# A two-block transformer kernel: order of the ScalarE and VectorE queues inside its two feed-forward stages

## The chip, the cores and the metric

The kernel runs on one core of one Trainium2 chip. The metric is the device time of one execution in microseconds (us), and the median of three runs is taken. TensorE multiplies, ScalarE (ACT in the profile), VectorE (DVE) and GpSimd (POOL) work elementwise, and SyncE (SP) issues most of the transfers. Each engine works through its own instruction queue in order, and the queues meet only at semaphores.

## The reference

Two transformer blocks work on 512 tokens of width 1024 (and 16 meta tokens), in float32. Each block has attention layers, an output projection and a feed-forward part. The change lies in the feed-forward part alone, which is the same in both blocks:

```
hn = rms_norm(h, g)
h  = h + (silu(hn @ w_gate) * (hn @ w_up)) @ w_down      # 1024 -> 2816 -> 1024
```

## The kernel before, in words

**Tiles.** Activations are kept with features on the 128 partitions and the 512 tokens along the free axis. The 2816 inner features are 22 tiles of 128, done in three parts of 8, 8 and 6 tiles (`FPARTS`): part a, b, c. After each part the product with `w_down` adds what the part gives to `hT` (phases `dn1a` and so on).

**Split operands.** A float32 product is done as three products of a rounded high half and a remainder: `wh` and `wl` of the weights, high and low half of the activations. ScalarE makes `wh` from the loaded weights in `stage` (`high`, L767). VectorE subtracts it to make `wl` (`low`, L1170). `stage`, `wh` and `wl` have two slots, b = 0 and 1. SyncE loads the next tile into a slot when `lo[b]` says that `wl` of the tile in it is made. TensorE starts `product(name, i, b)` (L1951) when `wl` of that tile is made and PSUM bank b has been read (`ev[b]`). ScalarE may overwrite `wh[b]` when the last product from it has ended (`mm[b]`).

**Ordinary tiles.** The first four inner tiles of part a in each block (`GATE_PLAIN`) are ordinary. Slot 0 holds the gate tile and slot 1 the up tile, and each product is 24 matmuls of 128x512. VectorE scales the gate product by the norm factor `R` (L1682), ScalarE takes the tanh (L1008), VectorE closes the silu (`opened`, L1649), scales the up product (L1654) and multiplies both (L1656). ScalarE makes the high half of the inner tile (`inner_high`, L995) and VectorE its low half (`inner_low`, L1661). In tile 0 the norm factor itself is made: VectorE waits for sums from TensorE, takes an inverse square root in small steps (L1600 to L1202) and builds four diagonals, from which TensorE spreads the factor.

**Gate pairs.** All other gate tiles are done in pairs (`gate_pair`, L1997), two gate tiles and then two up tiles; there are 2, 4 and 3 pairs in parts a, b and c, so 18 in both blocks. The two gate tiles over two halves of the tokens are multiplied by a scheme with seven half products instead of eight. It uses sums of weight tiles (`weight_sums`, L1627 to L1631, split by `sum_high` L979 and `sum_low` L1639) and sums of token halves (`token_sum` L1610, split by `token_sum_high` L990 and `token_sum_low` L1617; four of them for each block, made while the ordinary tiles run, into two scratch tiles `ta` and `tb`). The order on TensorE of the half products, each 12 matmuls of 128x256, is in this text x1, w, z, y1, x2, y2, x3. The banks x and y (`psS` 0 and 2) are used again within a pair, so ScalarE has to copy their interim sums out: `part_x` after x1 (L1032) and after x2 (L1040), `part_z` after z (L1035) and after y1 (L1038). y2 waits for the copy made after y1 (`out_y`), and x3 for the copy made after x2 (`out_x`). Then follow the two up tiles as ordinary products. `second_high` (L985) and `second_low` (L1644) are the second half of the split of a pair's second gate tile.

**The queue of ScalarE in a pair before the change:**

```python
act.activation(part_x[:, 0:HT], psS[:, 0, 0:HT], ACT.Copy).then_inc(out_x, 1)    # after x1
high(name, i + 1, 0)                                                             # first up tile
act.activation(part_z[:, 0:HT], psS[:, 3, 0:HT], ACT.Copy).then_inc(out_z, 1)    # after z
high(name, i + 1, 1)                                                             # second up tile
act.wait_ge(acc_y, 2 * n + 1)
act.activation(part_z[:, HT:], psS[:, 2, 0:HT], ACT.Copy).then_inc(out_y, 1)     # after y1
act.wait_ge(acc_x, 3 * n + 2)
act.activation(part_x[:, HT:], psS[:, 0, 0:HT], ACT.Copy).then_inc(out_x, 1)     # after x2
```

The order of all of this is written out by hand, in `swiglu` of the scalar block (L997) and `swiglu` of the vector block (L1663).

Of the kernel before, what the change touches and what calls it, by code (L numbers as in the profile page):

```python
# [235 lines left out]
def build(nc, t, out):  # L236
    with ExitStack() as ctx:
# [150 lines left out]
        ft, o = at("ft", [P, 5, SEQ], o)  # L388
# [366 lines left out]
        def _(act):  # L755
# [241 lines left out]
            def swiglu(l, part):  # L997
                name, f0, pairs_ = f"gu{l}{'abc'[part]}", before_part(l, part), gate_pairs(l, part)
                plain = GATE_PLAIN[part]
                for i in range(plain):  # L1000
                    high(name, i, 1)
                    if i == 0:
                        high_next(name, i, False)
                    if i == 1:
                        token_sum_high(l, 0)
                        token_sum_high(l, 1)
                    act.wait_ge(ev[0], PAIR0[name] + i + 1)
                    act.activation(ft[:, 1, :], ft[:, 0, :], ACT.Tanh, scale=0.5).then_inc(t_ok, 1)  # L1008
                    if i:
                        high_next(name, i, False)  # L1010
                    if i == 1:
                        token_sum_high(l, 2)
                        inner_high(i, f0)
                    elif i == 2:
                        token_sum_high(l, 3)
                        inner_high(i, f0)
                    elif i == plain - 1:
                        sum_high(pairs_[0][1], 0)
                        second_high(name, pairs_[0][0])
                        inner_high(i, f0)  # L1020
                        sum_high(pairs_[0][1], 1)
                    else:
                        inner_high(i, f0)
                if not plain:
                    sum_high(pairs_[0][1], 0)
                    second_high(name, pairs_[0][0])
                    sum_high(pairs_[0][1], 1)

                for i, n in pairs_:
                    last = i == pairs_[-1][0]  # L1030
                    act.wait_ge(acc_x, 3 * n + 1)
                    act.activation(part_x[:, 0:HT], psS[:, 0, 0:HT], ACT.Copy).then_inc(out_x, 1)  # L1032
                    high(name, i + 1, 0)
                    act.wait_ge(mm[1], PAIR0[name] + i + 1)
                    act.activation(part_z[:, 0:HT], psS[:, 3, 0:HT], ACT.Copy).then_inc(out_z, 1)  # L1035
                    high(name, i + 1, 1)
                    act.wait_ge(acc_y, 2 * n + 1)
                    act.activation(part_z[:, HT:], psS[:, 2, 0:HT], ACT.Copy).then_inc(out_y, 1)  # L1038
                    act.wait_ge(acc_x, 3 * n + 2)
                    act.activation(part_x[:, HT:], psS[:, 0, 0:HT], ACT.Copy).then_inc(out_x, 1)  # L1040
                    act.wait_ge(gate_ok, 2 * n + 1)
                    act.activation(ft[:, 1, :], ft[:, 0, :], ACT.Tanh, scale=0.5).then_inc(t_ok, 1)
                    act.wait_ge(gate_ok, 2 * n + 2)
                    act.activation(tanh2[:], ft[:, 2, :], ACT.Tanh, scale=0.5).then_inc(t_ok, 1)
                    if not last:
                        sum_high(n + 1, 0)
                    high_next(name, i + 1, last)
                    inner_high(i, f0)
                    if not last:
                        sum_high(n + 1, 1)  # L1050
                        second_high(name, i + 2)
                    inner_high(i + 1, f0)
# [9 lines left out]
            name = "dn1c"  # L1062
# [44 lines left out]
            for j in range(len(units) + 6):  # L1107
# [4 lines left out]
                if j in Y_NORM:  # L1112
                    i = Y_NORM.index(j)
# [18 lines left out]
            name = "dn2c"  # L1132
# [24 lines left out]
        def _(v):  # L1157
# [490 lines left out]
                v.wait_ge(t_ok, f0 + i + 1)  # L1648
                dv.link(v.scalar_tensor_tensor(out=gated, in0=tanh, scalar=1.0, in1=gated, op0=ALU.add, op1=ALU.mult))  # L1649

            def times_up(name, i, b, up, f0, gated):

                done(name, up, b)
                v.tensor_tensor(ft[:, 3, :], psL[:, b, :], R, ALU.mult).then_inc(ev[b], 1)  # L1654
                v.wait_ge(ev[b], PAIR0[name] + up + 1)
                v.scalar_tensor_tensor(out=ft[:, 4, :], in0=gated, scalar=0.5, in1=ft[:, 3, :], op0=ALU.mult, op1=ALU.mult).then_inc(hid_ok, 1)  # L1656

# [5 lines left out]
            def swiglu(l, part, head=None):  # L1663
                name, f0, pairs_ = f"gu{l}{'abc'[part]}", before_part(l, part), gate_pairs(l, part)
                first, pair0 = pairs_[0]
                for i in range(first):
                    low(name, i, 1)
                    if i == 0:
                        new_rms(head[0])
                        diagonals(diag, rs[:, 0:4]).then_inc(diag_ok, 1)  # L1670
                        low_next(name, i, False)
                        v.wait_ge(bcast, head[1])
                        v.tensor_copy(R, psT[:, 1, :]).then_inc(R_ok, 1)
                        v.wait_ge(R_ok, head[1])
                    if i == 1:
                        token_sum(l, 0)
                        token_sum(l, 1)
                    elif i == 2:
                        token_sum_low(l, 1)
                        token_sum(l, 3)  # L1680
                    done(name, i, 0)
                    v.tensor_tensor(ft[:, 0, :], psL[:, 0, :], R, ALU.mult).then_inc(ev[0], 1)  # L1682
                    if i:
                        low_next(name, i, False)
                    opened(i, f0, ft[:, 0, :], ft[:, 1, :])
                    if i == 1:
                        token_sum_low(l, 0)
                        token_sum(l, 2)
                    elif i == 2:
                        token_sum_low(l, 2)  # L1690
                        token_sum_low(l, 3)
                    elif i == first - 1:
                        weight_sums(name, first, pair0)
                        sum_low(pair0, 0)
                        second_low(name, first)
                    times_up(name, i, 1, i, f0, ft[:, 0, :])
                    inner_low(i, f0)
                    if i == first - 1:
                        sum_low(pair0, 1)

                for i, n in pairs_:
                    last = i == pairs_[-1][0]
                    done(name, i, 0)
                    v.wait_ge(out_x, 2 * n + 1)
                    v.tensor_tensor(ft[:, 0, 0:HT], psS[:, 1, 0:HT], part_x[:, 0:HT], ALU.add).then_inc(ev[0], 1)
                    low(name, i + 1, 0)
                    low(name, i + 1, 1)
                    v.wait_ge(acc_y, 2 * n + 2)
                    v.wait_ge(out_x, 2 * n + 2)
                    dv.link(v.tensor_tensor(ft[:, 0, HT:], psS[:, 2, 0:HT], part_x[:, HT:], ALU.add))  # L1710
                    v.tensor_tensor(ft[:, 0, :], ft[:, 0, :], R, ALU.mult).then_inc(gate_ok, 1)
                    v.wait_ge(acc_x, 3 * n + 3)
                    v.wait_ge(out_y, n + 1)
                    v.wait_ge(out_z, n + 1)
                    v.tensor_tensor(ft[:, 2, :].rearrange("p (a t) -> p a t", a=2), psS[:, 0, 0:HT].unsqueeze(1).broadcast_to([P, 2, HT]),
                                    part_z[:].rearrange("p (a t) -> p a t", a=2), ALU.add).then_inc(ev[1], 1)
                    v.wait_ge(ev[1], PAIR0[name] + i + 1)
                    v.tensor_tensor(ft[:, 2, :], ft[:, 2, :], R, ALU.mult).then_inc(gate_ok, 1)
                    v.wait_ge(gate_ok, 2 * n + 2)
                    opened(i, f0, ft[:, 0, :], ft[:, 1, :])  # L1720
                    opened(i + 1, f0, ft[:, 2, :], tanh2[:])
                    if not last:
                        weight_sums(name, i + 2, n + 1)
                    times_up(name, i, 0, i + 1, f0, ft[:, 0, :])
                    low_next(name, i + 1, last)
                    if not last:
                        sum_low(n + 1, 0)
                    inner_low(i, f0)
                    if not last:
                        sum_low(n + 1, 1)  # L1730
                    times_up(name, i + 1, 1, i + 1, f0, ft[:, 2, :])
                    if not last:
                        second_low(name, i + 2)
                    inner_low(i + 1, f0)
# [750 lines left out]
```

## Time and profile before

| | |
|---|---|
| median of three runs | 1555.14 us (1549.74 to 1555.39) |
| the profiled execution, its own time | 1557.15 us |
| its span, first to last instruction | 1555.4 us |
| TensorE busy with matmuls, with weight loads | 97%, 81% |
| VectorE, ScalarE, GpSimd busy | 62%, 39%, 16% |
| mean granted TensorE clock | 0.994 |

Busy time is the time in which an engine works on instructions. The idle time before an instruction is put down to what released it. Matmuls are pipelined and the ends that the profile gives for them are modelled, so starts are the safer reading.

### The profile page before, as it was taken

To read this page: it belongs to the slowest core of one execution; us is meant where nothing else is said; L and a number is where in the kernel's file an instruction comes from. 1 tells how busy PE (TensorE), PEld (TensorE's weight loads), DVE (VectorE), ACT (ScalarE), POOL (GpSimd) and SP (SyncE) were. 2 spreads that over 40 slices of the span, in tenths; PEclk is the share of its full clock that TensorE was granted. 3 is DMA by queue.
4 is the path that set the end of the run, shared out by engine and by line. 5 is a ranking of instruction groups with operands and counts; after the bars stand their busy time and mean duration, and the time that the engine had idled before them with its cause. 6 is when DMAs were issued, how large, how long until landed. Compare 5 with 4: busy or idle time off the path is not lost.

```text
span 1555.4 us, 21898 instructions
## 1 busy us (share of the span) xinstructions
PE 1508.1 (97%) x8004; PEld 1253.4 (81%) x8004; DVE 968.6 (62%) x1698; ACT 607.0 (39%) x1061; POOL 241.9 (16%) x206
## 2 busy tenths in 40 slices
PE   7999999999989999999999999999999999999998
PEld 6878886877778888888799778788777788888886
DVE  5578795466676477476854283544657855863764
ACT  5134445524433244243511374444343423432433
POOL 2323334340000000000002553222400000000000
PEclk9999999999999999999999999999999999999999
DMA  6524420033333333332323202111332233333322
GB/s 150 150 56 150 124 55 1 8 100 99 92 95 88 99 91 104 95 96 85 91 82 86 63 1 82 55 57 38 104 93 86 85 103 107 87 95 95 109 68 95
DMA packets 250308, 132.96 MB, mean 85 GB/s; under 512 B 21226, under 2 KB 247654, under 8 KB 250223
## 3 DMA queue, kind: packets, MB, share of 16 engines
q1 hardware_dynamic: 247998, 123.92, 28.0%
q0 software_dynamic: 2144, 7.77, 1.6%
q8 instruction: 54, 0.88, 0.2%
q14 instruction: 32, 0.25, 0.1%
q10 hardware_dynamic: 80, 0.14, 0.0%
HBM read 129.67 MB, written 6.38 MB: 87 GB/s over the span
## 4 chain that ended last, share of the span: by engine, by line
PE 77%; DVE 10%; DMA 6%; ACT 4%; issue 2%; POOL 0%; SPq 0%; DVEq 0%; ACTq 0%; POOLq 0%
PE psL L1971 44%; PE psL L2151 11%; PE psS L1971 5%; PE psS L1994 4%; DMA stage<-in_w_ffn_up 2%; ACT wh L767 2%; PE psT L2160 2%; DMA stage<-in_w_ff_up 2%; PE psS L2407 1%; DVE wl L1170 1%; PE psL L2279 1%; PE psS L2430 1%; DVE ft L1654 1%; PE psS L2256 1%; DVE ft L1656 1%
## 5 line engine op out<-in xcount | busy, mean ns | idle before, releaser
L767 ACT ACTIVATE wh<-stage 128x1024 fp32r<-128x1024 f32 (+3 forms) x232 | 225.3, 971 | 378.3 <-PE psL L1971 248.6
L1971 PE MATMUL psL<-hn,wh 128*128 128x512 f32 x1104 | 350.3, 399 | 7.9 <-DVE wl L1170 7.3
L1971 PEld LDWEIGHTS psL<-hn,wh 128*128 128x128 f32 x1104 | 204.1, 188 | 59.2 <-DVE wl L1170 11.4
L1170 DVE TENSOR_TENSOR wl<-stage,wh 128x1024 fp32r<-128x1024 f32 (+1 forms) x151 | 180.3, 1194 | 81.0 <-ACT wh L767 80.8
L1971 PE MATMUL psL<-hid,wh 128*128 128x512 f32 x704 | 221.6, 395 | 1.2 <-DVE wl L1170 1.2
L1971 PE MATMUL psL<-hn,wl 128*128 128x512 f32 x552 | 217.3, 394 | 0.0
L617 POOL TENSOR_TENSOR wl<-stage,wh 128x1024 fp32r<-128x1024 f32 (+2 forms) x81 | 154.4, 1907 | 306.9 <-ACT wh L767 306.9
L2151 PE MATMUL psL<-hn,wh 128*128 128x512 f32 x496 | 173.0, 430 | 0.4 <-DVE yn L1885 0.4
L1971 PEld LDWEIGHTS psL<-hid,wh 128*128 128x128 f32 x704 | 131.3, 187 | 35.2 <-DVE wl L1170 2.8
L1971 PE MATMUL psL<-hid,wl 128*128 128x512 f32 x352 | 138.8, 394 | 0.0
L1971 PEld LDWEIGHTS psL<-hn,wl 128*128 128x128 f32 x552 | 103.9, 188 | 23.8
L2151 PEld LDWEIGHTS psL<-hn,wh 128*128 128x128 f32 x496 | 88.7, 189 | 19.3 <-DVE yn L1885 0.8
L2151 PE MATMUL psL<-hn,wl 128*128 128x512 f32 x248 | 97.9, 395 | 0.0
L1739 DVE TENSOR_TENSOR hT<-hT,psL 128x512 f32 (+1 forms) x48 | 32.9, 686 | 93.7 <-PE psL L1971 93.6
L1971 PE MATMUL psS<-hn,wh 128*128 128x264 f32 x448 | 87.3, 296 | 0.7 <-DVE hn L1220 0.7
L1971 PE MATMUL psL<-mix,wh 128*128 128x512 f32 x256 | 81.0, 397 | 1.2 <-DVE wl L1170 1.2
L1994 PE MATMUL psS<-xt,wsh 128*128 128x256 f32 x432 | 79.5, 283 | 0.2
L1971 PEld LDWEIGHTS psL<-hid,wl 128*128 128x128 f32 x352 | 65.9, 187 | 16.1
L1971 PEld LDWEIGHTS psS<-hn,wh 128*128 128x128 f32 x448 | 73.1, 197 | 2.5 <-issue 1.2
L689 POOL MEMSET m8d<- 128x128 f32 x1 | 0.2, 213 | 441.2 <-DVE kaT L1297 441.2
L1994 PEld LDWEIGHTS psS<-xt,wsh 128*128 128x128 f32 x432 | 67.0, 191 | 0.7 <-ACT part_x L1032 0.7
L1971 PE MATMUL psS<-hn,wl 128*128 128x264 f32 x224 | 65.6, 293 | 0.0
(428 smaller groups left out, 2704.9 us busy)
## 6 DMA issues: line engine op xcount, KB each, us to landing
stage<-in_w_in SPq DMA_DIRECT2D x54, 512.0 KB, 3.8
stage<-in_w_ffn_gate SPq DMA_DIRECT2D x22, 512.0 KB, 3.8
stage<-in_w_ffn_up SPq DMA_DIRECT2D x22, 512.0 KB, 3.9
stage<-in_w_ff_gate SPq DMA_DIRECT2D x22, 512.0 KB, 3.8
stage<-in_w_ff_up SPq DMA_DIRECT2D x22, 512.0 KB, 3.9
stage<-in_w_out SPq DMA_DIRECT2D x16, 512.0 KB, 3.8
stage<-in_w_ffn_down SPq DMA_DIRECT2D x16, 512.0 KB, 3.8
stage<-in_w_ff_down SPq DMA_DIRECT2D x16, 512.0 KB, 3.7
```

The source lines that it names most:

```text
L617: pool.tensor_tensor(wl[:, b, 0:n], stage[:, b, 0:n], wh[:, b, 0:n].bitcast(F32), ALU.subtract).then_inc(lo[b], 1)
L767: act.activation(wh[:, b, 0:n], stage[:, b, 0:n], ACT.Copy).then_inc(hi[b], 1)
L1170: v.tensor_tensor(wl[:, b, 0:n], stage[:, b, 0:n], wh[:, b, 0:n].bitcast(F32), ALU.subtract).then_inc(lo[b], 1)
L1654: v.tensor_tensor(ft[:, 3, :], psL[:, b, :], R, ALU.mult).then_inc(ev[b], 1)
L1656: v.scalar_tensor_tensor(out=ft[:, 4, :], in0=gated, scalar=0.5, in1=ft[:, 3, :], op0=ALU.mult, op1=ALU.mult).then_inc(hid_ok, 1)
L1739: v.tensor_tensor(hT[:, n, :], hT[:, n, :], psL[:, b, :], ALU.add).then_inc(ev[b], 1)
L1971: ins = pe.matmul(dst, w[:, b, k * P:(k + 1) * P], x[:, part, k, c0:c1], start=k + n == 0, stop=k == kc - 1 and n == 2)
L1994: ins = pe.matmul(dst, w[:, cols], x(part, k), start=not add and k + n == 0, stop=k == KD // 2 - 1 and n == 2, skip_group_check=True)
L2151: ins = pe.matmul(psL[:, b, :], w[:, b, k * P:(k + 1) * P], hn[:, part_, k, META:], start=k + n == 0, stop=k == KD - 1 and n == 2)
L2160: ins = pe.transpose(psT[:, n % 2, m * P:(m + 1) * P], tile[:, col:col + P], ident[:])
L2256: ins = pe.matmul(psS[:, 2 * (j % 2) + bank, 0:k1 - k0], q, kz[:, h, k0:k1], start=True, stop=True)
L2279: ins = pe.matmul(psL[:, i % 2, h * HD:(h + 1) * HD], PT[:, n % 2, m * P:(m + 1) * P], vB[:, c, h * HD:(h + 1) * HD], start=h == 0 and m = ...
```

## The change

Three things are reordered, and no instruction is added or taken away. In a gate pair, ScalarE makes the copy after y1 ahead of the split of the second up tile. In the ordinary tiles, the split of the next up tile (`high(name, i + 1, 1)` and `low(name, i + 1, 1)`) stands ahead of the halves of the inner tile, on VectorE between L1654 and L1656 (`between`), and the split of the next gate tile stands ahead of the tanh. The token sums and the work for the first pair are laid out anew around that: the first token sum moves into tile 0, ahead of the norm factor.

```diff
             def swiglu(l, part):                          # scalar block
                 name, f0, pairs_ = f"gu{l}{'abc'[part]}", before_part(l, part), gate_pairs(l, part)
                 plain = GATE_PLAIN[part]
+                if plain:
+                    high(name, 0, 1)
+                    high_next(name, 0, False)
                 for i in range(plain):
-                    high(name, i, 1)
-                    if i == 0:
+                    if i:
                         high_next(name, i, False)
-                    if i == 1:
-                        token_sum_high(l, 0)
-                        token_sum_high(l, 1)
                     act.wait_ge(ev[0], PAIR0[name] + i + 1)
                     act.activation(ft[:, 1, :], ft[:, 0, :], ACT.Tanh, scale=0.5).then_inc(t_ok, 1)
-                    if i:
-                        high_next(name, i, False)
+                    if i < 2:
+                        token_sum_high(l, i)
+                    elif i == 2:
+                        token_sum_high(l, 3)
+                    if i < plain - 1:
+                        high(name, i + 1, 1)
+                    else:
+                        sum_high(pairs_[0][1], 0)
+                        second_high(name, pairs_[0][0])
+                        sum_high(pairs_[0][1], 1)
                     if i == 1:
                         token_sum_high(l, 2)
-                        inner_high(i, f0)
-                    elif i == 2:
-                        token_sum_high(l, 3)
-                        inner_high(i, f0)
-                    elif i == plain - 1:
-                        sum_high(pairs_[0][1], 0)
-                        second_high(name, pairs_[0][0])
-                        inner_high(i, f0)
-                        sum_high(pairs_[0][1], 1)
-                    else:
-                        inner_high(i, f0)
+                    inner_high(i, f0)
...
                     act.activation(part_z[:, 0:HT], psS[:, 3, 0:HT], ACT.Copy).then_inc(out_z, 1)
-                    high(name, i + 1, 1)
                     act.wait_ge(acc_y, 2 * n + 1)
                     act.activation(part_z[:, HT:], psS[:, 2, 0:HT], ACT.Copy).then_inc(out_y, 1)
+                    high(name, i + 1, 1)
                     act.wait_ge(acc_x, 3 * n + 2)
...
-            def times_up(name, i, b, up, f0, gated):      # vector block
+            def times_up(name, i, b, up, f0, gated, between=None):

                 done(name, up, b)
                 v.tensor_tensor(ft[:, 3, :], psL[:, b, :], R, ALU.mult).then_inc(ev[b], 1)
+                if between:
+                    between()
                 v.wait_ge(ev[b], PAIR0[name] + up + 1)
...
                 for i in range(first):
-                    low(name, i, 1)
                     if i == 0:
+                        low(name, i, 1)
+                        token_sum(l, 0)
                         new_rms(head[0])
...
-                    if i == 1:
-                        token_sum(l, 0)
+                    elif i == 1:
                         token_sum(l, 1)
                     elif i == 2:
                         token_sum_low(l, 1)
-                        token_sum(l, 3)
+                    elif i == 3:
+                        token_sum_low(l, 3)
                     done(name, i, 0)
                     v.tensor_tensor(ft[:, 0, :], psL[:, 0, :], R, ALU.mult).then_inc(ev[0], 1)
...
                         token_sum_low(l, 0)
                         token_sum(l, 2)
                     elif i == 2:
+                        token_sum(l, 3)
                         token_sum_low(l, 2)
-                        token_sum_low(l, 3)
                     elif i == first - 1:
                         weight_sums(name, first, pair0)
                         sum_low(pair0, 0)
                         second_low(name, first)
-                    times_up(name, i, 1, i, f0, ft[:, 0, :])
-                    inner_low(i, f0)
+                    times_up(name, i, 1, i, f0, ft[:, 0, :], (lambda: low(name, i + 1, 1)) if i < first - 1 else None)
                     if i == first - 1:
                         sum_low(pair0, 1)
+                    inner_low(i, f0)
```

## Rows read from the trace of the kernel before

**Rows 1.** The page: span, and busy time by engine.
```profile
span 1555.4 us, 21898 instructions
PE 1508.1 (97%) x8004; PEld 1253.4 (81%) x8004; DVE 968.6 (62%) x1698; ACT 607.0 (39%) x1061; POOL 241.9 (16%) x206
```

**Rows 2.** Waits of PE and of PEld, whole run: us in total, times, longest us.
```profile
PE psS L1994 <- ACT part_z L1038: 10.9, 17, 1.6
PE psL L1971 <- DVE wl L1170: 9.7, 11, 1.6
...
PEld psS L1994 <- ACT part_x L1032: 0.7, 2, 0.3
```

**Rows 3.** Waits of PE, 398.4 to 449.8, then 1170.05 to 1221.45: ordinary tiles.
```profile
PE psL L1971 <- DVE wl L1170: 3.6, 3, 1.6
...
PE psL L1971 <- DVE wl L1170: 3.7, 4, 1.6
```

**Rows 4.** Timeline of ACT, a later pair: start us, us, work, [idle before <-releaser].
```profile
479.57 1.06 ACT L767 ACTIVATE wh<-stage 128x1024 fp32r<-128x1024 f32 x1 [1.29 <-DMA stage<-in_w_ffn_up]
480.53 0.36 ACT L1038 ACTIVATE part_z<-psS 128x256 f32<-128x256 f32 x1
480.79 0.38 ACT L1040 ACTIVATE part_x<-psS 128x256 f32<-128x256 f32 x1
```

**Rows 5.** Timeline, same pair: DVE's `wl`; first starts of x1, x2; x2's last matmul; y2.
```profile
469.50 1.22 DVE L1170 TENSOR_TENSOR wl<-stage,wh 128x1024 fp32r<-128x1024 f32 x1
...
473.52 0.39 PE L1994 MATMUL psS<-hn,wh 128*128 128x256 f32 x2
...
479.13 0.40 PE L1994 MATMUL psS<-xt,wsh 128*128 128x256 f32 x2
...
480.45 0.28 PE L1994 MATMUL psS<-xt,wsl 128*128 128x256 f32 x1
481.04 0.47 PE L1994 MATMUL psS<-hn,wsh 128*128 128x256 f32 x2 [0.31 <-ACT part_z L1038]
481.35 0.28 PE L1994 MATMUL psS<-hn,wsl 128*128 128x256 f32 x1
```

**Rows 6.** Timeline, last ordinary tile: its gate product, and the chain to the up product.
```profile
436.91 0.73 PE L1971 MATMUL psL<-hn,wh 128*128 128x512 f32 x2
...
441.46 0.63 ACT L995 ACTIVATE hid<-ft 128x512 fp32r<-128x512 f32 x1 [4.92 <-DVE ft L1656]
442.00 1.04 ACT L767 ACTIVATE wh<-stage 128x1024 fp32r<-128x1024 f32 x1
442.35 0.40 PE L1971 MATMUL psL<-hn,wl 128*128 128x512 f32 x1
443.08 1.23 DVE L1170 TENSOR_TENSOR wl<-stage,wh 128x1024 fp32r<-128x1024 f32 x1 [0.26 <-ACT wh L767]
444.36 0.73 PE L1971 MATMUL psL<-hn,wh 128*128 128x512 f32 x2 [1.61 <-DVE wl L1170]
444.93 0.39 PE L1971 MATMUL psL<-hn,wl 128*128 128x512 f32 x1
```

**Rows 7.** Timeline of DVE, tile 0: the idle time ahead of the norm factor.
```profile
405.64 0.16 DVE L1600 TENSOR_SCALAR st<-psT 128x4 f32<-128x4 f32 x1 [2.25 <-PE psT L2032]
```

**Rows 8.** Line of DVE, weight sums: xcount | busy us, mean ns | idle before.
```profile
L1627 DVE TENSOR_TENSOR wsum<-stage 128x512 f32<-128x512 f32 x18 | 12.4, 691 | 0.9 <-DMA stage<-in_w_ff_gate 0.5
```

**Rows 9.** Page: up loads, us to landing. Then timeline, first pair of part b.
```profile
stage<-in_w_ffn_up SPq DMA_DIRECT2D x22, 512.0 KB, 3.9
...
539.57 2.35 SPq L496 DMA_DIRECT2D stage<-in_w_ffn_up  x2
546.86 1.06 ACT L767 ACTIVATE wh<-stage 128x1024 fp32r<-128x1024 f32 x1 [2.20 <-DMA stage<-in_w_ffn_up]
```

**Rows 10.** Windows: us, PE, PEld, DVE, ACT, POOL busy (x), PEclk, DMA share, GB/s.
```profile
775.00:778.40 3.40, 3.15 (x27) 2.94 (x27) 2.36 (x2) 1.11 (x2) 0.00 (x0) 1.00 0.00 0
778.40:781.90 3.50, 3.50 (x18) 3.50 (x18) 2.86 (x18) 0.00 (x0) 0.00 (x0) 0.51 0.54 154
```

## The prediction

> **What bounds the kernel now.** I read the page first: TensorE is busy for 97% of the span and no other engine for more than 62% [rows 1]. So the time is TensorE's work plus TensorE's gaps, and a reordering without new instructions can win back gaps only. The view of waits, for TensorE alone, says where they are: the two longest entries are 10.9 us in 17 gaps until the copy of `part_z` at L1038, and 9.7 us in 11 gaps until a `wl` tile of L1170 [rows 2]. The first belongs to the gate pairs, of which there are 18. For the second I asked the same view for the two stretches of ordinary tiles: 3.6 us in 3 gaps and 3.7 us in 4 [rows 3]. The rest of the 9.7 us lies in phases that the change doesn't touch.
>
> The timelines show why. In a pair, ScalarE gets to the split of the second up tile (L767) at 479.57, when its weights land, and the copy that y2 needs (L1038) stands behind it and runs from 480.53 [rows 4]. ScalarE had 1.29 us of idle time just before [rows 4]. TensorE ends x2 and gets to y2 at 481.04, 0.31 us of idle time late [rows 5]. In an ordinary tile, TensorE's next up product waits for a chain: the inner tile's high half at 441.46, the weights' split at 442.00, `wl` at 443.08, the product at 444.36 [rows 6]. Only the last two links are needed for the product. The first, and the VectorE work that it waited for, stand ahead of them by order of the queue alone.
>
> **What a gap costs.** The recorded idle time is too small a measure. In the pair, the last matmul of x2 starts at 480.45 and y2 at 481.04, 0.59 us, where 48 matmuls from 473.52 to 479.13 make 0.117 us each; the next start but one is 0.31 instead of 0.23 us on [rows 5]. The gap of 0.31 us thus cost 0.47 + 0.08 = 0.55 us, or 0.24 more than recorded. In the ordinary tile the starts are 2.01 us apart, and 0.57 for the next two matmuls [rows 6]; the gate product before has 23 steps in 442.35 - 436.91 = 5.44 us, 0.236 each [rows 6]. The cost is 2.01 - 0.24 + 0.57 - 0.47 = 1.87 us for 1.61 us of idle time, 0.26 more. The Trainium skill (Perfetto Trace Analysis, Identifying the Most-Contended Engine) says the same of the sum: matmul busy time hides headroom because matmuls are pipelined, and the busy share of weight loads should be read instead. By that rule the headroom would be 19% and not 3% [rows 1]; as a sum it gives nothing here, since it doesn't say which part is waiting.
>
> **Part 1, the copy ahead of the split, 18 pairs.** Removed: 17 gaps, 10.9 + 17 x 0.24 = 15.0 us. Moved: one ScalarE copy of 0.36 us; no transfer is issued from ScalarE's queue. What comes next: y1's 12 matmuls are the ones before x2's first at 479.13 [rows 5], with a tail of 0.28 us after the last one's start, so the copy can run at about 479.4 to 479.8. The split of the up tile then starts at 479.8 instead of 479.57 and ends at 480.9. The copy after x2 follows and is done by 481.3. TensorE, no longer held, starts y2 at 480.57 and x3 at 482.0. So 0.7 us of slack is left in a later pair. `wl` of the second up tile comes 0.25 us later, but its product stands behind x3 and a product of 5.6 us, some 7 us away (482.2 against 489.1): nothing. The only other one that waits for it is SyncE, with the load of the next pair's second gate tile, which the weight sums want. Loads have held those up for 0.5 us in all 18 [rows 8]; 0.25 us more in each would hardly be felt, since the next pair's first `wl` ends at 470.7 and the pair begins at 473.52 [rows 5], 2.8 us of cover.
>
> The late case is the first pair of a part, where both up tiles are loaded together: issued from 539.57 on, the second is split at 546.86, 7.3 us later, where two issues 2.0 us apart and the usual 3.9 us to landing would make 5.9 [rows 9]. In parts b and c the pair begins about 0.2 us after that issue. The split ends at 547.9, the copy after x2 at 548.3, and x3 is wanted 6 x 1.41 = 8.5 us into the pair, at 548.3: 0 to 0.3 us is left of a wait. I take 0.2 us for all four together, since the usual landing is 1.4 us sooner.
>
> **Part 2, ordinary tiles, 4 in each block.** Let E be the end of an up product. ScalarE splits the next up tile from E + 0.2 to E + 1.25 (1.04 us [rows 6]), VectorE does L1654 (0.69 us) in that time and then `wl` until E + 2.5 (1.23 us [rows 6]). TensorE wants it at E + 5.6, after the gate product. The slack is 3 us. The gate tile's split goes ahead of the tanh: ready 2.5 us after its product's end, wanted 5.6 after. So the 7 gaps recorded go, 3.6 + 3.7 [rows 3], with 7 x 0.26 more, and 0.4 us for the fourth of the first block, which is too short there to be listed (I put it at 0.1 us): 7.3 + 1.8 + 0.4 = 9.5 us. The gap of 0.2 us at the start of tile 1, until the scaling at L1682, stays.
>
> Is VectorE's queue too full for this? The heaviest tiles (1 and 2) hold two splits of weights and three instructions for token sums, of the same shape, 1.23 us each [rows 6], and five of 128x512, 0.69 us each [rows 8]: 6.2 + 3.5 = 9.7 us in a period of two products, 11.2. It fits. The first token sum (1.23 us) moves to tile 0, where VectorE stands idle for 2.25 us until 405.64 [rows 7]: 1.0 us of that cover is left; if it were gone, the norm factor and with it the gap at L1682 would grow by what is missing. In tile 3, from the gate product's end G: scaling and `wl` until G + 2.5, silu until 3.2, four weight sums of 0.69 us [rows 8] until 6.0, `wsl` until 7.2, second half of the second gate tile until 7.9. The pair begins at G + 5.6 and z wants that at G + 8.4. It fits with 0.5 us.
>
> The up tiles of this pair are loaded from the end of the weight sums on, 0.4 us into the pair. With 5.9 to 7.3 us for two loads [rows 9], 1.04 for the split and 0.6 for the copy and its signal, the copy after x2 is ready 7.9 to 9.3 us in, and x3 wants it at 8.5: 0 to 0.8 us, plus 0.24, for 2 pairs. I take 0.35 each, 0.7 together. Against it the two waits for the first copy of `part_x` go, 0.7 us [rows 2], since the inner tile's high half, which stood ahead, comes sooner.
>
> **Sum.** 15.0 + 9.5 + 0.7 - 0.2 - 0.7 = 24.3 us. The profiled execution took 1557.15 us (its span of 1555.4 and 1.7 around it), so 1532.8 for it. The median stands 2.0 us below that, at 1555.14, which gives **1530.8 us**.
>
> **The rivals.** *The recorded idle time is all there is.* The modelled ends could be right, and the 0.24 and 0.26 us be something that stays. Then 10.9 + 7.3 come back: 1537. The starts speak against it, 5%.
> *The wait moves on to the copy after x2.* It now stands behind the split at L767 as the other did, and x3 waits for it. Needed: weights that land 0.7 us later in a pair than in [rows 4]. If it took all of part 1: 1555.1 - 9.5 = 1545.6. 5%.
> *The ordinary tiles give nothing back*, since a token sum or the weight sums land ahead of a `wl` tile in a queue that is 9.7 of 11.2 us full. Then only part 1: 1540. 6%.
> *The change doesn't do what it says*: ScalarE still gets to the copies late in the pairs, and the ordinary tiles find another wait of the same size. 1552 to 1556, 4%.
> *Slower.* The split of the second up tile now waits for y1 too, and TensorE's last product of the pair waits for that split. It decides only if the split comes over 7 us later than now; then each of 18 pairs pays what is over. To be 0.5% slower the pairs would have to give back 25 us and cost 8 more, 1.8 us each beyond that slack: 1563 or more. No row has a landing near that late. 1%, and 1% for a fault that I don't see.
>
> **TensorE's clock** is inside the forecast. From 778.4 to 781.9 the granted clock was 0.51, so 1.2 GHz instead of 2.4, and 18 matmuls were recorded where a stretch as long before it had 27 [rows 10]. I estimate up to 1.7 us for it, half of the 3.5, in stages that the change only moves in time. One of the three runs was 5.4 us shorter than the other two, which such spells could make. The Trainium skill (TensorE: Matmul & The Clock Gate, Part 1) says that the monitor behind this clock runs freely and doesn't start with the kernel, so its spells vary from run to run. The one trace can't show that.
>
> **How the numbers follow.** A measurement of this kernel tells about 0.5%, 7.8 us, from no change. The forecast has 78%: 1530.8, with 6 us down for the clock and 5 us up for residual waits and the clock, so 1525 to 1536. To hold 8 in 10 with the cases at 1537 and 1540 I take 1524 to 1541, which leaves out the rivals at 1545 and above. Faster by over 0.5% (below 1547.4) are the forecast and the first three rivals, 94%; within it 4%; slower 2%.
>
> **What would show it.** Right: no wait of TensorE for `part_z` in the list, none for a `wl` tile in the ordinary tiles, except 0.2 us for L1682; a stretch of ordinary tiles shorter by 4.7 us; L1038 ahead of the second L767 of each pair. The residual: waits for `part_x` at L1040, in few first pairs. Wrong: a new entry for `part_x` with a count near 18, `wl` still listed in the ordinary tiles, the norm factor later than now, or z waiting for L1644.

## The result, and the profile after

| | kernel before | changed kernel |
|---|---|---|
| median of four runs | 1555.27 us (1549.74 to 1557.01) | 1532.86 us (1531.81 to 1533.57) |
| the profiled execution, its own time | 1557.15 us | 1533.0 us |
| its span | 1555.4 us | 1530.9 us |

The ratio of the changed kernel to the one before is 0.9861, with a 95% interval of 0.9836 to 0.9887. The forecast was 1530.8 us in a range of 1524 to 1541, so it missed by 2.1 us.

The page of the changed kernel: span, then busy time by engine, then the chain that ended last, by engine.

```profile
span 1530.9 us, 21900 instructions
...
PE 1502.8 (98%) x8004; PEld 1255.0 (82%) x8004; DVE 966.5 (63%) x1698; ACT 609.8 (40%) x1061; POOL 242.1 (16%) x206
...
PE 92%; DVE 4%; issue 1%; DMA 1%; ACT 1%; SPq 0%; POOL 0%; DVEq 0%; ACTq 0%; POOLq 0%
```

Beside [rows 1] the counts of instructions on TensorE, VectorE, ScalarE and GpSimd are the same and their busy times move by less than 6 us each. The work is what it was, and the gaps are gone.

Waits of TensorE, changed kernel, whole run: us in total, times, longest us. (`wl` is made at L1167 here, L1170 before.)

```profile
PE psS L2060 <- DMA xin<-in_x: 5.3, 2, 2.8
PE psT L2041 <- POOL ones L590: 2.9, 1, 2.9
PE psL L1971 <- DVE wl L1167: 2.1, 4, 0.6
...
PE psL L1971 <- DVE ft L1682: 0.4, 2, 0.2
```

The 17 waits for `part_z` and the 2 for `part_x` of [rows 2] are in no line any more. Of the 11 waits for a `wl` tile 4 are left; they start at 354.51, 730.35, 1112.18 and 1487.86, so at the start of an output projection or of a `dn1c` or `dn2c`, phases that the change doesn't touch. What [rows 3] answers to is one line. The same view for the ordinary tiles alone, 396.0 to 449.9:

```profile
PE psL L1971 <- DVE ft L1682: 0.2, 1, 0.2
```

The chain of work that ended last, in the changed kernel over that stretch and the first pairs: start us, us, what.

```profile
412.80 33.60 PE psL L1971 x144
446.40 9.90 PE psS L1994 x84
456.30 11.13 PE psL L1971 x48
467.44 9.90 PE psS L1994 x84
```

From the start of tile 1 on the chain never leaves TensorE. Here is what that makes in lengths, start to start of the first matmul of a stage (us). "Pairs" are the parts a, b and c from the first matmul of their first pair to the first of their `w_down` product:

| stage | before | changed |
|---|---|---|
| ordinary tiles, first and second block | 51.63, 51.66 | 46.68, 46.67 |
| pairs, first block | 45.07, 87.36, 65.86 | 42.08, 84.37, 63.12 |
| pairs, second block | 45.17, 86.00, 64.95 | 42.14, 84.16, 63.12 |
| first feed-forward product starts at | 398.40 | 399.56 |

The ordinary tiles gave 9.9 us, the pairs 394.4 - 379.0 = 15.4 us, 25.4 together before rounding. The span is 24.5 us shorter, because the profiled execution reached the first feed-forward product 1.2 us later. Nothing ahead of it was changed. In the profiled kernels below that also change nothing there, that start lies between 395.99 and 400.84.

The mechanism in the pair is seen best where [rows 4] and [rows 5] showed the stall. Timeline of ScalarE in the same pair of the changed kernel: start us, us, work, [idle before <-releaser].

```profile
470.34 1.06 ACT L767 ACTIVATE wh<-stage 128x1024 fp32r<-128x1024 f32 x1 [0.51 <-PE psS L1994]
471.64 0.39 ACT L1032 ACTIVATE part_z<-psS 128x256 f32<-128x256 f32 x1 [0.24 <-PE psS L1994]
473.08 0.38 ACT L1034 ACTIVATE part_z<-psS 128x256 f32<-128x256 f32 x1 [1.05 <-PE psS L1994]
473.36 1.05 ACT L767 ACTIVATE wh<-stage 128x1024 fp32r<-128x1024 f32 x1
474.52 0.38 ACT L1037 ACTIVATE part_x<-psS 128x256 f32<-128x256 f32 x1
```

The copy after y1 (L1034) now waits for TensorE and for no transfer. The split follows at 473.36, and then the copy after x2 (L1037). TensorE in the same pair, with the last matmul of x2, the first of y2 and the first of x3:

```profile
474.20 0.28 PE L1994 MATMUL psS<-xt,wsl 128*128 128x256 f32 x1
474.32 0.40 PE L1994 MATMUL psS<-hn,wsh 128*128 128x256 f32 x2
...
475.75 0.40 PE L1994 MATMUL psS<-xt,wsh 128*128 128x256 f32 x2
```

y2 starts 0.12 us after the last matmul of x2, the pace of the half products, where [rows 5] had 0.59. The copy after x2 ends at 474.90, 0.85 us ahead of x3.

In the ordinary tiles [rows 6] had `wl` behind the inner tile. VectorE in tile 1 of the changed kernel, and TensorE's product from that `wl`:

```profile
423.36 1.22 DVE L1607 TENSOR_TENSOR ta<-hg,tb 128x1024 f32<-128x1024 f32 x1
424.62 0.69 DVE L1651 TENSOR_TENSOR ft<-psL,Rk 128x512 f32<-128x512 f32 x1
425.35 1.23 DVE L1167 TENSOR_TENSOR wl<-stage,wh 128x1024 fp32r<-128x1024 f32 x1
426.49 0.69 DVE L1655 SCALAR_TENSOR_TENSOR ft<-ft 128x512 f32<-128x512 f32 x1
```

```profile
429.56 0.62 PE L1971 MATMUL psL<-hn,wh 128*128 128x512 f32 x2
```

`wl` is ready at 426.58 and its product starts at 429.56. That is a slack of about 3.0 us in the fullest of the tiles.

### The profile page after: what moved, and what is told of

Its sections match the earlier page's. It is cut to its first block, busy times and chain, and to the rows that moved or that the text cites. A ratio compares the mean times of both kernels' runs of the same rounds, so it can differ in the third digit from the quotient of the medians.

```text
span 1530.9 us, 21900 instructions
## 1 busy us (share of the span) xinstructions
PE 1502.8 (98%) x8004; PEld 1255.0 (82%) x8004; DVE 966.5 (63%) x1698; ACT 609.8 (40%) x1061; POOL 242.1 (16%) x206
## 4 chain that ended last, share of the span: by engine, by line
PE 92%; DVE 4%; issue 1%; DMA 1%; ACT 1%; SPq 0%; POOL 0%; DVEq 0%; ACTq 0%; POOLq 0%
PE psL L1971 50%; PE psS L1994 12%; PE psL L2151 11%; PE psS L1971 5%; PE psT L2160 2%; PE psS L2407 1%; PE psL L2279 1%; PE psS L2430 1%; PE psS L2256 1%; PE psS L2186 1%; PE psL L2384 1%; DMA xin<-in_x 1%; PE psS L2199 1%; PE psS L2363 1%; PE psS L2364 1%
## 5 line engine op out<-in xcount | busy, mean ns | idle before, releaser
L1167 DVE TENSOR_TENSOR wl<-stage,wh 128x1024 fp32r<-128x1024 f32 (+1 forms) x151 | 180.3, 1194 | 75.3 <-ACT wh L767 75.0
```

The source lines that it names most:

```text
L1167: v.tensor_tensor(wl[:, b, 0:n], stage[:, b, 0:n], wh[:, b, 0:n].bitcast(F32), ALU.subtract).then_inc(lo[b], 1)
```

## Experiments

The questions were: do both halves of the change bring what was put down for them (1, 2); is a gap's true cost larger than its recorded idle time (2, 5); how far are the new waits from deciding (3 to 7, 10); and is there more to have (9). In this order, each with what was on record before it ran. Kernels of one group ran on one chip beside the kernel before: 1, 2 and 3; then 4, 5, 6 and 7; then 8, 9 and 10. Lengths of stages come from the one profiled execution of each kernel. The two of the changed kernel (the result and 8) agree to 0.05 us in the ordinary tiles and to 0.02 in the sum of the pairs, and to 0.2 in a single part.

**1. Only the pairs.** The kernel before, with the copy after y1 put ahead of the split.

```diff
-                    high(name, i + 1, 1)
                     act.wait_ge(acc_y, 2 * n + 1)
                     act.activation(part_z[:, HT:], psS[:, 2, 0:HT], ACT.Copy).then_inc(out_y, 1)
+                    high(name, i + 1, 1)
```

> The kernel before with the copy after y1 ahead of the split of the second up tile, and nothing else. My theory (a gap costs its recorded idle time plus about 0.24 us of slower starts): 15.0 us less than before for the 17 gaps, so about 1540, and no wait of TensorE for part_z left; the seven waits for wl in the ordinary tiles stay. Rival (only the recorded idle time comes back): 10.9 us less, 1544. Rival (the wait moves on to the copy after x2): near 1555, with some 17 waits for part_x.

Measured: 1539.98 us (1538.88 to 1546.39) against 1555.33, ratio 0.9914 (0.9894 to 0.9934). The ordinary tiles stay at 51.67 and 51.64 us. The pairs take 43.25, 84.16, 63.12, 44.06, 84.16 and 63.46, which is 382.2, or 12.2 us less than before. Waits of TensorE in this kernel:

```profile
PE psL L1971 <- DVE wl L1170: 9.9, 12, 1.6
...
PE psS L1994 <- DVE wl L1644: 0.9, 1, 0.9
```

No `part_z` is left in the list, as predicted. The median met the expected 1540, but by stages the gain is 12.2 us and not 15.0, so part of that hit is luck. Parts a are 1.2 and 1.9 us longer than in the whole change. Of this, 0.75 us in each first pair is no price of the new order: the wait for the first `part_x` [rows 2] is still there, and x2 starts 6.1 us into the pair instead of 5.6. The rest lies in the second pairs, where z comes late, once with 0.9 us of wait for `second_low` (L1644). The line of the weight sums shows what stands ahead of that: xcount | busy us, mean ns | idle before.

```profile
L1627 DVE TENSOR_TENSOR wsum<-stage 128x512 f32<-128x512 f32 x18 | 12.4, 691 | 5.0 <-DMA stage<-in_w_ff_gate 3.6 <-DMA stage<-in_w_ffn_gate 1.1
```

In [rows 8] this idle time was 0.9 us. The split is not later than before, though. In the first pair of the second block's part a it starts 7.4 us after the pair's first matmul (7.9 before), and the sums start 15.6 us after it (15.8 before). But TensorE is no longer held ahead of y2, and the pair lasts 21.8 us instead of 23.4. What hangs on the loads (the split, `wl`, `lo[1]`, SyncE's load of the next second gate tile, the sums, `second_low`) did not get faster by as much, so z now meets it. In the whole change the ordinary tiles' new order has the loads of the up tiles issued 0.4 us into that pair instead of 1.1, the sums start at 13.7, and no z waits.

**2. Only the ordinary tiles.** The changed kernel, with the edit of 1 taken out again.

> The changed kernel with the copy after y1 put back behind the split. My theory: 9.5 us less than before plus what goes in the first pairs, so about 1545, both stretches of ordinary tiles 4.7 us or more shorter, and 17 or 18 waits for part_z as before, the first ones of part a shorter. Rival (recorded idle time alone): 7.3 us less, 1548. If the two parts don't depend on each other, the gains of this kernel and of the pairs alone add up to that of the whole change, 24 to 25 us of span.

Measured: 1543.8 us (1542.04 to 1545.44), ratio 0.993 (0.9915 to 0.9946). The ordinary tiles take 46.69 and 46.68 us, all that the whole change gives there. The pairs take 392.2, 13.2 us more than in the changed kernel. Its waits of TensorE have

```profile
PE psS L1994 <- ACT part_z L1035: 9.6, 17, 1.4
```

This is the cleanest measurement of what a gap costs, because one order in one queue separates the two kernels: 13.2 us for 17 gaps of 9.6 us recorded, (13.2 - 9.6) / 17 = 0.21 us more for each. By stages 1 gives 12.2, and 2 gives 9.9 + 2.2 = 12.1, together 24.3 against 25.4 for both at once. By medians it is 15.4 + 11.5 = 26.9 against 22.4. The medians scatter by more than what they would have to tell, and I go by the stages.

**3. Both copies ahead of the split.**

```diff
                     act.wait_ge(acc_y, 2 * n + 1)
                     act.activation(part_z[:, HT:], psS[:, 2, 0:HT], ACT.Copy).then_inc(out_y, 1)
-                    high(name, i + 1, 1)
                     act.wait_ge(acc_x, 3 * n + 2)
                     act.activation(part_x[:, HT:], psS[:, 0, 0:HT], ACT.Copy).then_inc(out_x, 1)
+                    high(name, i + 1, 1)
```

> The changed kernel with the copy after x2 ahead of the split of the second up tile too, so the split starts about 1.3 us later in each pair. My theory: its product is wanted some 7 us later, so no time is lost and the same as the changed kernel comes out, 1533, within 0.5 us of span. The rival of the prediction on the slower side (the held-back split becomes the wait) would need more than 7 us; if it held at this distance, 18 pairs would show a wait for wl and 5 us or more.

Measured: 1533.7 us (1531.31 to 1536.31), ratio 0.9862 (0.9842 to 0.9883), so not to be told from the change by its time. The stages tell more: the pairs take 381.6 us, 2.6 more than in the changed kernel, where I had put at most 0.5. In the first pair of part b in the second block, TensorE starts at 1292.48 here and at 1290.84 in the changed kernel. The split of the second up tile starts 7.5 us into the pair instead of 6.1. VectorE in this kernel from there on, the three rows that follow from that split:

```profile
1301.09 1.23 DVE L1167 TENSOR_TENSOR wl<-stage,wh 128x1024 fp32r<-128x1024 f32 x1 [2.79 <-ACT wh L767]
...
1307.11 0.69 DVE L1624 TENSOR_TENSOR wsum<-stage 128x512 f32<-128x512 f32 x1 [0.95 <-DMA stage<-in_w_ff_gate]
...
1316.44 0.68 DVE L1641 TENSOR_TENSOR wl<-stage,wh 128x512 fp32r<-128x512 f32 x1
```

and TensorE's z in the next pair:

```profile
1317.18 0.50 PE L1994 MATMUL psS<-xt,wh 128*128 128x256 f32 x2 [0.69 <-DVE wl L1641]
```

In the changed kernel the same three of VectorE are

```profile
1298.01 1.23 DVE L1167 TENSOR_TENSOR wl<-stage,wh 128x1024 fp32r<-128x1024 f32 x1 [1.36 <-ACT wh L767]
...
1303.85 0.69 DVE L1624 TENSOR_TENSOR wsum<-stage 128x512 f32<-128x512 f32 x1
...
1313.41 0.68 DVE L1641 TENSOR_TENSOR wl<-stage,wh 128x512 fp32r<-128x512 f32 x1
```

Counted from the start of the pair, `wl` is 8.6 - 7.2 = 1.4 us later, the sums 14.6 - 13.0 = 1.6 and `second_low` 24.0 - 22.6 = 1.4, and z is held up by 0.69 us recorded. It starts 0.97 us after the matmul ahead of it, where 0.11 is usual, and its pair lasts 22.05 us instead of 21.04. So of 1.4 us of delay about 0.5 is covered here and the rest reaches TensorE, where I had counted on "some 7 us". This is the worst place. The same shift made the other eleven pairs that follow a pair 0.1 to 0.45 us longer, so most of it was covered there. The six first pairs, which follow no pair, did not get longer.

**4 and 5. More on ScalarE between the split and the copy after x2**: in 4 the first, in 5 all three of these idle copies of 128x512 into scratch tiles.

```diff
                     high(name, i + 1, 1)
+                    act.activation(sq[:], R, ACT.Copy)
+                    act.activation(tmp[:, 0, :], R, ACT.Copy)
+                    act.activation(tmp[:, 1, :], R, ACT.Copy)
                     act.wait_ge(acc_x, 3 * n + 2)
```

> The changed kernel with one useless ScalarE copy of 128x512 in every pair, between the split of the second up tile and the copy after x2, which delays that copy by about 0.53 us. The slack that I read is 0.7 us in later pairs and less in first ones. My theory: no wait in the 12 later pairs, 0 to 0.7 us in some of the 6 first pairs, in all 0 to 3 us over the changed kernel. If there were no slack, 18 waits for part_x of 0.5 us and with the slower starts 13 us.

> The same with three such copies, so the copy after x2 comes about 1.6 us later. My theory: 1.6 - 0.7 = 0.9 us of idle time in the 12 later pairs and 1.0 to 1.6 in the 6 first ones, with 0.24 us of slower starts each: 12 x 1.14 + 6 x 1.5 = 23 us over the changed kernel, 18 waits for part_x. If a gap cost only its recorded idle time: 18 to 19 us.

Measured: 1532.23 us for one and 1548.92 us for three, single runs, with 1554.45 for the kernel before beside them. With one, the pairs take 380.0 us, 1.0 more than in the changed kernel (0.8 of it in the two parts a), and no wait for `part_x` is listed. With three they take 393.3, 14.3 more, where I expected 23. Waits of TensorE with three:

```profile
PE psS L1997 <- ACT part_x L1040: 10.0, 18, 1.3
```

ScalarE with three, same later pair as above, then TensorE's x3:

```profile
475.61 1.06 ACT L767 ACTIVATE wh<-stage 128x1024 fp32r<-128x1024 f32 x1
476.58 0.62 ACT L1036 ACTIVATE sq<-Rk 128x512 f32<-128x512 f32 x1
477.10 0.62 ACT L1037 ACTIVATE tmp<-Rk 128x512 f32<-128x512 f32 x1
477.62 0.61 ACT L1038 ACTIVATE tmp<-Rk 128x512 f32<-128x512 f32 x1
478.14 0.36 ACT L1040 ACTIVATE part_x<-psS 128x256 f32<-128x256 f32 x1
```

```profile
478.55 0.50 PE L1997 MATMUL psS<-xt,wsh 128*128 128x256 f32 x2 [0.51 <-ACT part_x L1040]
```

Three copies add 3 x 0.52 = 1.56 us, and a pair is longer by 14.3 / 18 = 0.79 on average, so the slack was about 0.8 us. The prediction's 0.7 was close. It isn't the same everywhere: x3 is late by 0.55 us in the pairs with most room and by 1.5 in the first pair of part b. My expectation for 5 was 9 us too high, and the 18 to 19 us of its rival were too high as well. About half of that is the 0.24 us of a gap, which I added on top of a delay that was already counted from start to start (18 x 0.24 = 4.3); the other half is more slack than I had put in, in the first pairs above all. The pair of numbers is a second measurement of a gap: 14.3 us for 10.0 recorded in 18 gaps, 0.24 more each. It also shows the rival "the wait moves on to the copy after x2" as real: 0.8 us away, and 0.8 us beyond it take back 14.3 of the 15.4 us.

**6. The first token sum back in tile 1.**

```diff
                     if i == 0:
                         low(name, i, 1)
-                        token_sum(l, 0)
                         new_rms(head[0])
...
                     elif i == 1:
+                        token_sum(l, 0)
                         token_sum(l, 1)
```

(and `token_sum_high` on ScalarE likewise)

> The changed kernel with the first token sum back in tile 1, on VectorE and ScalarE. Its cover in tile 0 is idle time, and tile 1 would then hold 11.0 us of VectorE work against 11.2. My theory: the scaling of tile 1 and all behind it come 1.2 us later, wl of the next up tile is then ready 1.4 us ahead of its product instead of 2.6, and nothing is lost: 0 to 1 us. Rival (the queue of VectorE is what ordinary tiles hang on): 1.2 us or more in each block, with a wait for wl in tile 2.

Measured: 1529.9 us, one run; ordinary tiles 46.69 and 46.72, the same. VectorE's idle time ahead of the norm factor, first in this kernel and then in the changed one:

```profile
404.63 0.16 DVE L1598 TENSOR_SCALAR st<-psT 128x4 f32<-128x4 f32 x1 [2.25 <-PE psT L2033]
```

```profile
406.87 0.16 DVE L1597 TENSOR_SCALAR st<-psT 128x4 f32<-128x4 f32 x1 [1.19 <-PE psT L2032]
```

The sum takes 1.06 us of an idle time of 2.25 and delays nothing. It also buys nothing: tile 1 has room for it.

**7 and 10. More on VectorE in tile 1**, right behind its last token sum: six, then twelve, idle copies of 128x512.

```diff
                         token_sum(l, 2)
+                        dv.link(v.tensor_copy(diag[:].rearrange("p n c -> p (n c)"), R))
+                        dv.link(v.tensor_copy(sq[:], R))
...
```

> The changed kernel with six useless VectorE copies of 128x512 ahead of the scaling of the up product in tile 1, 4.5 us in each block. My theory, from the changed kernel's timeline: wl of the next up tile would end at about 431.1 instead of 426.6 and is wanted at 428.6, so one wait of 2.5 us in each block, nothing in the tiles behind: 5.5 us over the changed kernel. If VectorE's queue had no slack: 9 us; if it had as much as the idle share of the whole stretch (18%, 9 us): nothing.

> The changed kernel with twelve useless VectorE copies ahead of the scaling of the up product in tile 1. With six, a copy took 0.46 us from start to start and not the 0.75 that I had put in, so 2.8 us in all, and wl of the next up tile ended some 0.2 us ahead of its product. Six more are 2.8 us more. My theory (slack of about 2.9 us and then one for one): 2.6 us and 0.25 of slower starts in each block, 5.6 us over the changed kernel, and both stretches of ordinary tiles 49.5 us. Rival (it is not this wait that such work meets first, or it spreads over the tiles behind): less than 1 us, or over 4 us in each block.

Measured, in single runs: with six 1531.19 us and 46.71, 46.69 in the ordinary tiles, no loss where I expected one of 5.5 us in all. With twelve 1540.06 us and 49.28, 49.32, so 2.6 more for each block, as expected the second time. VectorE with six:

```profile
421.88 0.43 DVE L1689 COPY diag<-Rk 128x512 f32<-128x512 f32 x1
422.35 0.43 DVE L1690 COPY sq<-Rk 128x512 f32<-128x512 f32 x1
...
424.66 0.69 DVE L1651 TENSOR_TENSOR ft<-psL,Rk 128x512 f32<-128x512 f32 x1
```

A copy of 128x512 takes 0.43 us, and the next starts 0.46 after its start. I had priced it like an operation with two operands, 0.69 us, and 0.75 from start to start. Six are 2.8 us, just inside the slack of 3.0 read above. Twelve are 5.6, and 5.6 - 3.0 = 2.6 us, which is what came. TensorE's wait with twelve:

```profile
432.27 0.50 PE L1983 MATMUL psL<-hn,wh 128*128 128x512 f32 x1 [2.33 <-DVE wl L1167]
```

So the slack of part 2, predicted as 3 us, is measured as 3.0. Both have a smaller price in part a of the pairs (43.1 to 43.4 us instead of 42.1, so 2.2 and 2.3 us in both blocks, which neither expectation had), where z waits for `second_low` (up to 0.49 us with twelve). That is the place that the prediction gave "0.5 us", and it is the tighter one: six copies cost something there and nothing in the ordinary tiles.

**8. The change again**, as the standard for 9.

> The changed kernel itself, for comparison on the same chip with the next two: about 1533, stretches of ordinary tiles of 46.7 us, pair parts of 42.1, 84.2 to 84.4 and 63.1 us. Its distance to the kernel before, by median, should be 22 to 24 us, that of the spans by stage 25.

Measured: 1530.44 us (1528.33 to 1532.74) against 1553.01 (1548.90 to 1556.99), ratio 0.9853 (0.983 to 0.9875).

**9. The four waits for `wl` that are left.** I took them to come from VectorE's clearing of `sqacc` (0.91 us) ahead of a split. In the changed kernel, at the one of 1487.86:

```profile
1486.08 0.91 DVE L1560 MEMSET sqacc<- 128x1024 f32 x1 [0.16 <-issue]
1486.91 0.90 DVE L1167 TENSOR_TENSOR wl<-stage,wh 128x768 fp32r<-128x768 f32 x1
```

The clearing is moved behind the weights' split in the attention branch, and into the last gate pair, where VectorE is idle:

```diff
+                    elif part == 2:
+                        clear_squares()
...
-            clear_squares()
             low("dn1c", 0, 1)
```

> The changed kernel with the clearing of sqacc (0.91 us on VectorE) moved from the start of the phases out1, out2, dn1c and dn2c, where it stands ahead of the first wl tile, into idle time of VectorE in the phase before. The changed kernel still has 4 waits for wl, 2.1 us, all there. My theory: they go, 2.1 us and 4 x 0.24 to 0.28 of slower starts, 3.1 us, so 1530. Rival (another wait takes their place at once, for instance for the split on ScalarE): 0 to 1 us.

Measured: 1528.45 us (1526.98 to 1529.14), ratio to before 0.984 (0.9818 to 0.9862), 2.0 us below 8. The waits of TensorE still have

```profile
PE psL L1972 <- DVE wl L1167: 1.1, 2, 0.7
```

The two in the `w_down` phases are gone, 0.6 us each, and from start to start these phases take 33.77 and 34.29 us instead of 34.45 and 34.90 in 8, 1.3 us less together. The two at the output projections (0.4 and 0.7 us here, 0.4 and 0.5 in the changed kernel) stay: the clearing was not what held them. So the stages show 1.3 us of the 3.1 expected. That the whole kernel is faster, by 2.0 us of median with ranges of runs that just overlap, is probable and not shown.

## Why the prediction was right

**The bound.** TensorE's work plus its gaps: right. The sum of stages fell by 25.4 us, the prediction had 24.3. The share of weight loads, which would have left 19%, doesn't measure gaps here: between 413 and 446 of the changed kernel no wait of TensorE is listed, and weight loads are busy for 26.73 of the 33 us, 81%.

**What a gap costs.** Predicted 0.24 us above the recorded idle time in a pair and 0.26 in an ordinary tile. Measured 0.21 (2 against the change) and 0.24 (5) in a pair, and 2.6 for 2.33 recorded in an ordinary tile, so 0.27 (10). The rival "recorded idle time is all there is" falls: it would give 9.6 and 10.0 us where 13.2 and 14.3 were measured.

**Part 1**, predicted 15.0 and, after the residual in first pairs, 14.8 (15.0 + 0.7 - 0.2 - 0.7): measured 15.4. From start to start the 15.4 are 14.6 for the `part_z` gaps (15.0 in the sum), 1.1 for the two waits for `part_x` (0.7) and 0.3 of new waits against them (0.2 + 0.7 = 0.9). The residual is the term that was mis-sized. I had x3 waiting 0.2 us in parts b and c, and 0.35 us in each part a. In the changed kernel no such wait is listed, and from start to start x3 was late once, by 0.10 us, in the first pair of part b. ScalarE in that pair:

```profile
540.30 1.06 ACT L767 ACTIVATE wh<-stage 128x1024 fp32r<-128x1024 f32 x1 [1.00 <-DMA stage<-in_w_ffn_up]
541.27 0.37 ACT L1037 ACTIVATE part_x<-psS 128x256 f32<-128x256 f32 x1
```

The split comes 540.30 - 533.12 = 7.2 us into the pair (7.0 in [rows 9]), so the landing was as late as the late end of my estimate, and the copy is done at 541.64, just as x3 starts (541.69). The other first pairs had more room.

**Part 2**, predicted 9.5: measured 4.95 + 4.99 = 9.9. Its slack, predicted 3 us, is 3.0 (7 and 10). The first token sum in tile 0 left 1.19 us of 2.25, predicted 1.0, and without it nothing changes (6). The gap at L1682 stayed at 0.2 us.

**The slack behind the split.** Predicted 0.7 us ahead of x3, measured 0.8 (5). Here the step that was right in its outcome was wrong in its reason. I wrote that `wl` of the second up tile has "some 7 us" before its own product wants it, and of its other consumer, SyncE, that 0.25 us "would hardly be felt". The second consumer is the tight one: 3 shows it at about 0.5 us in a first pair, through `lo[1]`, the load of the next second gate tile, the weight sums, `second_low` and z, a whole pair further on. In the other later pairs about 1 us or more was covered. In the changed kernel the weight sums wait 1.4 us in two places, instead of the 0.5 of [rows 8], and no z is held up. But the rival "slower" was priced with a threshold of 7 us, and z begins to pay at 0.5 to 1.3. It stayed unlikely for another reason: the copy is held back only by TensorE's own pace, so the split moves by a fraction of a microsecond. In the pair of [rows 4] it started 6.05 us into the pair before and starts at 6.08 now.

**The ordinary tiles give nothing back**: refuted by 2 alone, 9.9 us. **The change doesn't do what it says**: refuted by the order in the timelines above. **The wait moves on**: not in the change, but with three copies it does (5).

**From the profiled execution to the median.** The sum for the profiled execution was 1532.8 and it took 1533.0. That they agree to 0.2 us is luck: the stages gave 1.1 us more than the sum had, and the first feed-forward product came 1.2 us later. I then took off 2.0 us, since the median of before stood so much lower than its profiled execution. In the changed kernel the two agree (1533.0 and 1532.86), so nearly all of the miss of 2.1 us is this offset; in 8 the median was 1530.44. The offset is scatter between executions. The start, above, moves by up to 5 us between the profiled kernels. TensorE's clock is the other source that the traces show. Windows of the changed kernel: us, PE, PEld, DVE, ACT, POOL busy (x), PEclk, DMA share, GB/s.

```profile
766.00:769.40 3.40, 3.40 (x17) 3.40 (x17) 2.82 (x18) 0.00 (x0) 0.00 (x0) 0.51 0.55 159
876.00:879.40 3.40, 3.40 (x14) 2.08 (x14) 2.87 (x8) 2.15 (x7) 1.69 (x2) 0.50 0.00 0
```

The first is the spell of [rows 10], in the same stage of the program and now 12 us earlier. Of the nine runs of the kernel before beside 8 to 10, the four with a mean granted clock of 0.998 or 0.999 took 1548.9 to 1552.7 us and the five with 0.993 to 0.996 took 1553.0 to 1557.0. So the two go together there. They don't in the changed kernel: of its four runs the one with the lowest mean clock, 0.992, was the fastest (1531.81), and the two with 0.995 were the slowest. How much of the scatter the spells make was not tried.

## What to carry to other kernels

In a hand-written in-order queue, look for an instruction that waits for a transfer and stands ahead of a short one that the bounding engine wants: 18 copies of 0.4 us, put ahead of splits that waited for DMA, gave 12.2 us alone and 13.2 on top of the other reordering. Price a gap by the distance of starts (here recorded idle time plus 0.21 to 0.27 us), and work out the slack of a delayed instruction for every consumer of what it frees. The one with 7 us hid one with 0.5 to 1.3, which went through a slot's semaphore, a load and the sums made from it. And look at what TensorE meets next once a wait is gone: in 1 the split and the sums came no later in their pair than before, and z waited all the same.

## What the hardware showed that I had not expected

VectorE copies 128x512 in float32 in 0.43 us, while its operations with two operands take 0.69 us on the same shape. The low granted clock (0.50 to 0.51, 1.2 GHz) comes at the same places of the program in different executions, though not at all of them in each: the window at 778 to 782 of the kernel before is the one at 766 to 769 of the changed one, while kernel 9 has the full clock all through that stage. The window of kernel 9 there, in the same columns:

```profile
764.40:767.80 3.40, 3.40 (x30) 3.40 (x30) 2.28 (x14) 0.44 (x1) 0.00 (x0) 1.00 0.56 159
```

There are 30 matmuls in it, where the changed kernel had 17. TensorE's work ahead of it is the same in all three, so that alone doesn't call the spell forth. Of the twelve traces of this case six have this spell, after 3920 to 3931 matmuls, and ten have the one at 876 of the changed kernel, after 4607 to 4609. Why those places, and why only in some executions, stays open.
